# A hybrid decoder step on one core: the split halves of the Strassen weight sums kept in DRAM by token group 0 and loaded by groups 1 to 3

## The reference

```python
def ffn_sublayer(x, g_pre, w_up_l, w_down_l, g_post):
    h = rmsnorm(x, g_pre)
    a = jax.nn.relu(jnp.einsum('btd,df->btf', h, w_up_l))
    return x + rmsnorm(jnp.einsum('btf,fd->btd', a * a, w_down_l), g_post)
```

## Time and profile before

| | |
|---|---|
| time, median of 3 runs | 2645.64 us (2641.29 to 2654.81) |
| the profiled execution: its own time / its span | 2644.41 us / 2642.6 us |
| mean granted TensorE clock | 0.984 of full speed |
| TensorE (matmul) busy | 2522.6 us, 95% of the span |
| VectorE, ScalarE, GpSimd busy | 1382.9, 1166.3, 1415.2 us |
| DMA | 457.65 MB, mean 173 GB/s |

### The profile page before, as it was taken

The page is one execution under the profiler, slowest core; times in us unless marked ns, Lnnn a source line. Parts: engine busy times, 40 slices in busy tenths (PEclk is TensorE's granted clock), DMA queues, the critical chain, the costliest instruction groups (busy, mean ns, idle before and its releaser), DMA issues.

```text
span 2642.6 us, 35400 instructions
## 1 busy us (share of the span) xinstructions
PE 2522.6 (95%) x13562; PEld 2167.4 (82%) x13562; DVE 1382.9 (52%) x2231; ACT 1166.3 (44%) x2002; POOL 1415.2 (54%) x818
## 2 busy tenths in 40 slices
PE   7999999999999999999998999998999999999995
PEld 6899999899996468778877788777778778889884
DVE  6431221265663225865566554676555476655657
ACT  4000110187775534545454444554544455444443
POOL 1216560068663566665566675666665475554555
PEclk9999999999999999999999999999999999999998
DMA  5316764299988944564556555456555263553452
GB/s 183 112 44 244 264 230 120 83 164 180 166 146 212 295 160 166 193 208 159 167 183 242 176 168 183 151 170 232 173 173 193 99 235 120 198 178 127 142 191 96
DMA packets 297903, 457.65 MB, mean 173 GB/s; under 512 B 81748, under 2 KB 202140, under 8 KB 290776
## 3 DMA queue, kind: packets, MB, share of 16 engines
q1 hardware_dynamic: 270546, 313.71, 41.3%
q10 hardware_dynamic: 14518, 89.43, 9.5%
q0 software_dynamic: 12672, 52.24, 5.9%
HBM read 390.50 MB, written 120.53 MB: 193 GB/s over the span
## 4 chain that ended last, share of the span: by engine, by line
PE 76%; DVE 10%; DMA 5%; POOL 3%; ACT 3%; issue 2%; SPq 0%; ACTq 0%; DVEq 0%; POOLq 0%
PE ml_y L2171 13%; PE ml_up L2095 8%; PE ml_up L2096 8%; PE ml_up L2097 8%; PE ml_y L2128 6%; PE pj_acc L518 6%; PE pj_acc L519 6%; PE pj_acc L520 6%; PE at_o L1187 5%; PE at_turn L1167 2%; POOL ml_w_lo L1983 2%; DVE ml_a_lo L2479 2%; DVE ml_a_lo_raw L2451 2%; DVE ml_w_lo L2485 2%; PE at_score L1156 2%
## 5 line engine op out<-in xcount | busy, mean ns | idle before, releaser
L1983 POOL TENSOR_TENSOR ml_w_lo<-em_raw,ml_w_hi 128x1024 fp32r<-128x1024 f32 x296 | 741.2, 2512 | 635.1 <-ACT ml_w_hi L2203 634.9
L2203 ACT CAST ml_w_hi<-em_raw 128x1024 fp32r<-128x1024 f32 x384 | 401.4, 1046 | 295.8 <-PE ml_y L2171 189.0
L2095 PE MATMUL ml_up<-ml_h_hi,ml_w_hi 128*128 128x512 f32 (+2 forms) x1280 | 457.1, 357 | 23.3 <-POOL ml_w_lo L1983 23.3
L2096 PE MATMUL ml_up<-ml_h_lo,ml_w_hi 128*128 128x512 f32 (+2 forms) x1280 | 453.5, 354 | 0.0
L2097 PE MATMUL ml_up<-ml_h_hi,ml_w_lo 128*128 128x512 f32 (+2 forms) x1280 | 452.6, 354 | 0.0
L2171 PE MATMUL ml_y<-ml_w_hi,ml_a_hi 128*128 128x512 f32 x896 | 358.2, 400 | 34.4 <-DVE em_hx L2513 13.8
L2171 PE MATMUL ml_y<-ml_w_lo,ml_a_hi 128*128 128x512 f32 x896 | 352.6, 393 | 0.0
L2171 PE MATMUL ml_y<-ml_w_hi,ml_a_lo 128*128 128x512 f32 x896 | 352.3, 393 | 0.0
L2095 PEld LDWEIGHTS ml_up<-ml_h_hi,ml_w_hi 128*128 128x128 f32 x1280 | 243.2, 190 | 66.3 <-POOL ml_w_lo L1983 35.3
L518 PE MATMUL pj_acc<-pj_h_hi,pj_w_hi 128*128 128x424 f32 (+1 forms) x800 | 290.3, 363 | 5.6 <-DVE pj_h_lo L736 5.6
L519 PE MATMUL pj_acc<-pj_h_lo,pj_w_hi 128*128 128x424 f32 (+1 forms) x800 | 283.5, 354 | 0.0
(11 more groups left out here) (319 smaller groups left out, 4559.8 us busy)
## 6 DMA issues: line engine op xcount, KB each, us to landing
em_raw<-in_w_up SPq DMA_DIRECT2D x64, 1024.0 KB, 6.2
em_raw<-scratch_wt SPq DMA_DIRECT2D x128, 512.0 KB, 4.7
em_raw<-in_w_down SPq DMA_DIRECT2D x96, 512.0 KB, 3.7
out_o_a_k_s<-in_cache_a_k ACTq DMA_DIRECT2D x8, 3060.0 KB, 11.9
out_o_a_v_s<-in_cache_a_v ACTq DMA_DIRECT2D x8, 3060.0 KB, 13.2
em_raw<-scratch_pt SPq DMA_DIRECT2D x34, 512.0 KB, 7.3
pj_work<-in_w_down POOLq DMA_DIRECT2D x16, 1024.0 KB, 6.3
scratch_wt<-pj_work POOLq DMA_DIRECT2D x16, 1024.0 KB, 4.5
```

Source lines behind the costliest of these rows:

```text
L1983: nc.gpsimd.tensor_tensor(split_of(w_lo, n), raw_of(n), f32(split_of(w_hi, n)), ALU.subtract).then_inc(w_lo_ready, 1)
L2095: pe.matmul(out, hi[:, k, :], h_hi[:, k, cols], start=(k == 0), stop=False)
L2096: pe.matmul(out, hi[:, k, :], h_lo[:, k, cols], start=False, stop=False)
L2203: nc.scalar.copy(split_of(w_hi, n), raw_of(n)).then_inc(w_hi_ready, 1)
```

## The change

In group 0 the four weight sums of a part are loaded and split as before, and SyncE then stores both halves of each in a new DRAM tensor `ws` (`save`: two DMAs of 512 KB for each of 32 units). In groups 1 to 3 the four sums of a part are not loaded from `wt` and not split: SyncE loads both halves from `ws` into the slots of `w_hi` and `w_lo` (`fetch`: two DMAs of 512 KB for each of 96 units), and TensorE waits for these DMAs. SyncE's list becomes one loop over all units: at unit n first the raw loads whose slot is freed by unit n or an earlier one, then `save(n)`, then `fetch(n + 2)`, which waits until TensorE has done unit n - 1. With the sums gone from `raw`, P1 and P2 of a part share one raw load in groups 1 to 3 and P3 has one of its own: four raw loads a part in place of six. `lo_by_dve` holds for group 0 alone, so that in groups 1 to 3 the `w_lo` of P3 is made by GpSimd. In group 0 a slot of `w_hi` and `w_lo` is written again only when its store has landed (`w_saved`).

```diff
--- before.py
+++ after.py
@@ -1604,8 +1604,10 @@
         kind, g, part, i = step
         if kind != "down" and i % 2 == 0:
             LOADS.append((step, (kind, g, part, i + 1)))
-        if kind == "down" and i in (P1, P2, P5):
+        if kind == "down" and g == 0 and i in (P1, P2, P5):
             LOADS.append((step, (kind, g, part, i + 1)))
+        if kind == "down" and g and i == P1:
+            LOADS.append((step, (kind, g, part, P2)))
         if kind == "down" and i == P3:
             LOADS.append((step,))
     for n, load in enumerate(LOADS):
@@ -1710,6 +1712,8 @@
         w_hi_ready = ph.sem("w_hi_ready")
         w_lo_ready = ph.sem("w_lo_ready")
         w_lo_by_dve = ph.sem("w_lo_by_dve")
+        w_saved = ph.sems("w_saved", SPLIT)
+        w_fetched = ph.sems("w_fetched", SPLIT)
         filled = ph.sem("filled")
         turn_hi = ph.sem("turn_hi")
         emptied = ph.sem("emptied")
@@ -1813,15 +1817,41 @@
 
         def lo_by_dve(n):
             kind, g, part, i = UNITS[n]
-            return kind == "down" and i in (LO_BY_DVE_LAST if part == LAST else LO_BY_DVE)
+            return kind == "down" and g == 0 and i in (LO_BY_DVE_LAST if part == LAST else LO_BY_DVE)
 
         DVE_LOS = [sum(lo_by_dve(m) for m in range(n + 1)) for n in range(NU)]
 
+        def fetched(n):
+
+            kind, g, part, i = UNITS[n]
+            return kind == "down" and g > 0 and i in SUM
+
+        def saved(n):
+
+            kind, g, part, i = UNITS[n]
+            return kind == "down" and g == 0 and i in SUM
+
+        HIS = [sum(not fetched(m) for m in range(n + 1)) for n in range(NU)]
+        FETCHES = [sum(fetched(m) for m in range(n % SPLIT, n + 1, SPLIT)) for n in range(NU)]
+        SAVES = [sum(saved(m) for m in range(n % SPLIT, n + 1, SPLIT)) for n in range(NU)]
+
+        def wait_hi(engine, n):
+            engine.wait_ge(w_hi_ready, HIS[n])
+
         def wait_lo(engine, n):
-            if lo_by_dve(n):
+            if fetched(n):
+                engine.wait_ge(w_fetched[n % SPLIT], 32 * FETCHES[n])
+            elif lo_by_dve(n):
                 engine.wait_ge(w_lo_by_dve, DVE_LOS[n])
             else:
-                engine.wait_ge(w_lo_ready, n + 1 - DVE_LOS[n])
+                engine.wait_ge(w_lo_ready, HIS[n] - DVE_LOS[n])
+
+        def wait_slot(engine, n):
+
+            if n >= SPLIT:
+                wait_used(engine, n - SPLIT)
+                if saved(n - SPLIT):
+                    engine.wait_ge(w_saved[n % SPLIT], 32 * SAVES[n - SPLIT])
 
         def wait_loaded(engine, load):
             engine.wait_ge(raw_in[load % RAW], LANDED[load])
@@ -1934,13 +1964,36 @@
             load_part(sp, d, early, MERGED_EARLY)
             load_part(sp, d, early, MERGED_EARLY + 1)
             load_convs(sp, 1)
-            for load in range(RAW, len(LOADS)):
-                load_raw(load)
-                if load == 4:
-                    sp.dma_start(gain_post[:], d["g_mix_post"].partition_broadcast(P)).then_inc(gain_in, 16)
-                    sp.dma_start(gain_pre[:], d["g_mlp_pre"].partition_broadcast(P)).then_inc(gain_in, 16)
-                if load == 8:
-                    sp.dma_start(gain[:], d["g_mlp_post"].partition_broadcast(P)).then_inc(const_in, 16)
+            def save(n):
+                kind, g, part, i = UNITS[n]
+                wait_hi(sp, n)
+                sp.dma_start(d["ws"][part, SUM[i], 0], f32(w_hi[:, n % SPLIT, :])).then_inc(w_saved[n % SPLIT], 16)
+                wait_lo(sp, n)
+                sp.dma_start(d["ws"][part, SUM[i], 1], f32(w_lo[:, n % SPLIT, :])).then_inc(w_saved[n % SPLIT], 16)
+
+            def fetch(n):
+                kind, g, part, i = UNITS[n]
+                wait_slot(sp, n)
+                if (g, part, i) == (1, 0, P7):
+                    for slot in range(SPLIT):
+                        sp.wait_ge(w_saved[slot], 32 * SAVES[NU - 1 - (NU - 1 - slot) % SPLIT])
+                sp.dma_start(f32(w_hi[:, n % SPLIT, :]), d["ws"][part, SUM[i], 0]).then_inc(w_fetched[n % SPLIT], 16)
+                sp.dma_start(f32(w_lo[:, n % SPLIT, :]), d["ws"][part, SUM[i], 1]).then_inc(w_fetched[n % SPLIT], 16)
+
+            load = RAW
+            for n in range(NU):
+                while load < len(LOADS) and UNIT_OF[LOADS[load - RAW][-1]] <= n:
+                    load_raw(load)
+                    if load == 4:
+                        sp.dma_start(gain_post[:], d["g_mix_post"].partition_broadcast(P)).then_inc(gain_in, 16)
+                        sp.dma_start(gain_pre[:], d["g_mlp_pre"].partition_broadcast(P)).then_inc(gain_in, 16)
+                    if load == 8:
+                        sp.dma_start(gain[:], d["g_mlp_post"].partition_broadcast(P)).then_inc(const_in, 16)
+                    load += 1
+                if saved(n):
+                    save(n)
+                if n + AHEAD < NU and fetched(n + AHEAD):
+                    fetch(n + AHEAD)
             for j in CLOSING_ORDER[0:2]:
                 load_res(sp, "x1", NG - 1, j)
             sp.wait_ge(early.merged, 2 * TILES)
@@ -1977,9 +2030,9 @@
                 nc.gpsimd.tensor_tensor(at, at, res[0:m, u % 2, :], ALU.add).then_inc(res_used, 1)
 
             def split_lo(n):
-                if n >= NU or lo_by_dve(n):
+                if n >= NU or lo_by_dve(n) or fetched(n):
                     return
-                pool.wait_ge(w_hi_ready, n + 1)
+                wait_hi(pool, n)
                 nc.gpsimd.tensor_tensor(split_of(w_lo, n), raw_of(n), f32(split_of(w_hi, n)),
                                         ALU.subtract).then_inc(w_lo_ready, 1)
 
@@ -2193,13 +2246,12 @@
         def _(act):
 
             def split_hi(n):
-                if n >= NU:
+                if n >= NU or fetched(n):
                     return
                 step = UNITS[n]
                 kind, g, part, i = step
                 wait_loaded(act, LOAD_OF[step])
-                if n >= SPLIT:
-                    wait_used(act, n - SPLIT)
+                wait_slot(act, n)
                 nc.scalar.copy(split_of(w_hi, n), raw_of(n)).then_inc(w_hi_ready, 1)
 
             def hi_mix(step):
@@ -2481,7 +2533,7 @@
             def split_lo(n):
                 if n >= NU or not lo_by_dve(n):
                     return
-                dve.wait_ge(w_hi_ready, n + 1)
+                wait_hi(dve, n)
                 nc.vector.tensor_tensor(split_of(w_lo, n), raw_of(n), f32(split_of(w_hi, n)), ALU.subtract).then_inc(w_lo_by_dve, 1)
 
             def lowered(frm):
@@ -3167,6 +3219,7 @@
 
 
 SCRATCH = {
+    "ws": (FF // P // 4, 4, 2, P, D),
     "pt": (FBLK, P, TOK),
     "kv": (TOK, D),
     "oct": (2, P, TOK),
```

## The result

The changed kernel takes 2696.6 us (median of 4 runs, 2687.16 to 2699.28), against 2646.07 for the kernel before: 1.0181 of it, 95% interval 1.0144 to 1.0217. It is slower by about 48 us, where I had forecast 10 us with a range to 2692. The profiled execution took 2687.16 us, span 2685.4; it is the shortest of the four, so its trace shows 43 of the 48 us.

What follows compares the result with a forecast made beforehand. TensorE was taken to set the end, its waits for VectorE and GpSimd being what can go. Costs of 45.4 us less 32 less 3 gave +10.4 on 2644.4: 2654.8, stated as 2656 us, range 2616 to 2692.

Steps and rivals of the forecast that it cites:

- the term of the saves: Group 0: 64 stores of 512 KB hold back ScalarE's casts three units later; 2 us, bounds 0 and 24.
- the rival of the saves: Group 0 stalls: casts held by `w_saved` until TensorE runs dry, 3 us in eight parts; 2675 us, chance 0.12.
- three signs of being wrong: P6 in parts 4 and 6 waits for nothing, odd parts wait as well, or group 0 becomes longer.
- The fetches: Loads of the stored halves that land late for TensorE: 12.2, 9.6, 4 and 5.6 us, plus 12 for the clock.
- 12 us for the clock: About six fetch waits as long as the one at 1518 us each lower the clock, costing 2 us more.
- P6 behind the copy: Even parts, groups 1 and 2: P6's fetch lands late behind the cache copy, 2.7 + 1.7 + 1.7 us a group, 12.2 us.
- Part 0 is spared: P6 of part 0 costs nothing extra behind the copy, as its residual wait is there already.
- P4: P4's fetch, last of five 1 MB loads, is late: 9.6 us in even parts, 4 us over ten parts.
- Part 7: Groups 1 and 2: P5's fetch stands behind P6's fetch and the next group's raw load; 2.8 us late, twice, 5.6.
- The queue is the bound: Rival: 1 MB takes 3.65 us, so P4 is late in nearly all 14 full parts; 2685 us, chance 0.16.
- The relief: Casts and splits dropped in groups 1 to 3 end TensorE's waits and clock lows, 32 us, plus 3 for GpSimd's short waits.
- hidden-fetches rival: Engines serve the fetch between the cache copy's rounds, so fetches land in time; 2620 us, chance 0.30.

Runs made afterwards that it cites:

- after_no_copies: The changed kernel with ScalarE's 16 cache copies left out, so two outputs are not written: 2624.01 us, 0.9926 of the kernel before.
- after_quarters: The changed kernel with each cache copy in four quarters of 765 KB, after up3 and P4 of every part: 2645.2 us, 1.0023 of before.
- relief_only: The changed kernel without stores and fetches; groups 1 to 3 neither load nor split the sums, TensorE multiplies leftover halves: 2615.74 us, 0.991 of before.

## Why the prediction was wrong

**What failed** is the term of the saves: "I take 2 us; the bounds are 0 and 3 us in each of eight parts, 24." It measures 27 us alone, over its own upper bound, and 32 to 35 us by the marks of group 0; the rival of the saves had the right mechanism (casts held by `w_saved` until TensorE runs dry), was given 0.12, and was priced from that bound. Of the prediction's three signs of being wrong two came true: group 0 is longer, and odd parts wait as well. Three things were wrong in the term.

First, I took one store's landing from a row in which nothing stood ahead of it, 2.8 us. In group 0 of the changed kernel the view of DMA issues, 1060 to 1400 us (KB each, median us to landing), has:

```profile
scratch_ws<-ml_w_hi SPq DMA_DIRECT2D x29, 512.0 KB, 7.5
scratch_ws<-ml_w_lo SPq DMA_DIRECT2D x29, 512.0 KB, 7.6
```

Second, I followed P6's and P4's stores and left out P7's, as if it were through before the copy. It has 1 MB of raw loads ahead of it in the same step of SyncE's list and is caught by the copy; `save_first`, which moves all stores ahead of the raw loads, removes that and 31 us with it. The copy is not the whole of it: without any copy group 0 is still 10.7 us longer, with quarters 28. Third, I counted the halves' slack (8.1 less 3.6 us) but not that ScalarE waits in order: VectorE's and GpSimd's work on the next operands waits with it, and every such stall of 4 us brings a low of the clock. In group 0 (1066 to 1410 us) the mean clock is 0.96, where it was 1.00.

**The fetches** were priced right in the sum, 43.4 us forecast (45.4 less the saves) and 36 to 41 measured, though not in place. That the sum came out is in part luck: P6 cost 9 us more than forecast, P4 and part 7 as much less. The 12 us for the clock were never measured by themselves, and the 11.3 us of waits in part 0, which the forecast does not have, come about in exchange for residual waits of 12. Beside part 0, TensorE's waits for fetches in groups 1 and 2 come to 31.8 us, where 31.4 was forecast (12.2 + 9.6 + 4 + 5.6):

- *P6 behind the copy*: right in mechanism. In part 2 of group 1 the chain has the fetch at 1541.55, 13.0 us to landing, and a wait of 4.8 us where I had 2.7; over parts 2, 4 and 6 of both groups it is 20.8 us, forecast 12.2. The data did not move at the rate I took: raw loads and `em_part` share them.
- *Part 0 is spared*: wrong in its reason. P6 waits 5.6 and 5.7 us there. The residual wait stands at up'1, behind P6, not ahead of it, and shrinks to 1.2 us or less once TensorE has already waited. The cost of part 0 is about nothing, as forecast.
- *P4*: 3.4 us in even parts, forecast 9.6, and 6.7 in odd ones, 4.6 of it in part 5, where the sum had 4 in ten parts and the list of signs none: the prediction contradicts itself there. Group 3, where it had no waits, has 2.7 us.
- *Part 7*: 0.5 and 0.4 us, forecast 2.8 each. The next group's raw load did not get ahead of P5's fetch as I had it. Why not, I have not tried.
- *The queue is the bound*: falls with after_no_copies, and with after_quarters, in which groups 1 and 2 are within 3 us of their base.

**The relief**: 35 us forecast (32 and 3), 24 measured, by the ratio; by the spans of the two profiled executions 30.5. The latter hold some 4 us from ahead of the last stage. So at most 11 us of the miss are here. About 9 of them are one term of the forecast with the wrong sign: I took 3 us off for the short waits for GpSimd's `w_lo`, "whose load falls by a tenth", and in `relief_only` they grew by 6 us. Why, no run shows. The 4.6 us of waits for adds that stay are the rest: not each of them had a `w_lo` to lose.

**Together**, then, a term of 27 in place of 2 and one of -24 in place of -35, beside the fetches' one (at most 41), which was nearly right, turn +10 into +44; 4 of the measured 48 us stay unexplained, less than the intervals of the runs.

**What the copy does to a fetch** was the crux of the hidden-fetches rival. The windows of 1 us of the changed kernel, where P6's fetch is issued at 1541.2 and 1541.6:

```profile
1541.00:1542.00 1.00, 0.82 (x4) 0.58 (x4) 1.00 (x2) 0.65 (x2) 1.00 (x2) 1.00 2.94 1044
1542.00:1543.00 1.00, 1.00 (x6) 0.82 (x5) 1.00 (x1) 0.00 (x0) 1.00 (x1) 1.00 0.00 0
1543.00:1544.00 1.00, 1.00 (x6) 0.81 (x6) 1.00 (x1) 0.00 (x0) 1.00 (x1) 1.00 0.00 0
1544.00:1545.00 1.00, 1.00 (x6) 0.84 (x5) 1.00 (x2) 0.00 (x0) 1.00 (x2) 1.00 2.78 979
...
1547.00:1548.00 1.00, 1.00 (x6) 0.84 (x5) 0.00 (x0) 0.78 (x2) 0.00 (x0) 1.00 0.58 205
```

A round is 16 transfers of 65280 bytes, 1044 KB, one on each engine. The second begins at 1541, the third at 1544, nearly 3 us after the fetch's issue, and in between nothing of the fetch begins. So the engines finish all three rounds first, and the fetch's data begin after 1547. The Trainium skill ("DMA: Bandwidth & Descriptors", section "Queues, rings and completion order") has an engine switch between queues only when it has drained a whole packet of several descriptors. I had taken each 65280-byte transfer for such a packet; the trace agrees with the page if the three that an engine has of a copy are one; that they are is inferred, no view shows a packet's bounds. That with rows of 4080 bytes the longest wait falls to 3.5 us speaks for it too.

## What to carry to other kernels

When a change stores a buffer that is used again at once, the store's landing becomes part of the buffer's cycle: price it with all that stands ahead of it in its queue and with the longest transfer that other queues can put in its way, not from a row in which it went alone. Try the order of issues early: here two moved lines were worth 31 us. Read a long DRAM-to-DRAM copy in a trace as a time in which nothing else starts; before putting new transfers on a hard deadline, cut the copy into pieces and put in the queue what is awaited ahead of what has slack. And two halves of a change that cancel in a stretch (here relief and fetches) can't be read from its length: run each alone.

## What the runs showed of the hardware

A copy of 3060 KB, issued in one piece, kept the 16 DMA engines for about 9 us (1538 to 1547 in part 2 of group 1) in which no transfer of the other queue began, even one issued nearly 3 us before the copy's last round. Cutting the same copies into quarters made the kernel before 0.55% faster by itself (0.9945). Short rows let the queues share, but the copy took 16 in place of 13 us to land. A store of 512 KB that lands in 2.8 us when nothing stands ahead of it took 7.5 us (median) in the busy queue and once 16.3. And the order of issues within one step of SyncE's list was worth 31 us.
